# A decoder step on one core: memory keys of the sample group turned through DRAM beside other stages, and two steps of the memory heads moved to ScalarE

## Chip, core and metric

One core of a Trainium2 chip runs the whole kernel. The metric is the device time of one execution in microseconds. TensorE (PE) multiplies, VectorE (DVE) and ScalarE (ACT) do elementwise work, GpSimd (POOL) adds squares and issues DMAs, SyncE (SP) issues the DMAs of the weights. PSUM holds eight banks, in two tensors of four: `acc` for products, `ab` for everything else.

## What is computed

A decoder step for 256 prompt tokens and 8 sample tokens (264 columns together), model width 2048, two layers: a pooling mixer, memory attention and a SwiGLU; then dilated attention, memory attention and a SwiGLU. This case is about the memory attention:

```python
def _mem_attend(h, mk, mv, w_q, w_o):
    n, length, _ = h.shape
    q = (h @ w_q).reshape(n, length, MEM_HEADS, MEM_HEAD_DIM)          # 4 heads of 128
    sc = jnp.einsum('nlhd,nmhd->nhlm', q, mk).astype(jnp.float32) * (MEM_HEAD_DIM ** -0.5)
    p = jax.nn.softmax(sc, axis=-1).astype(mv.dtype)                   # over 256 memory rows
    o = jnp.einsum('nhlm,nmhd->nlhd', p, mv).reshape(n, length, MEM_DIM)
    return o @ w_o
```

It is called once with the prompt's memory keys, which the kernel computes itself, and once with `cache_mem_k[l]`, eight batches of 256 rows x 4 heads x 128 read from DRAM. The scores contract over the 128 of a head, so the cached keys, which lie as rows, are needed turned: 128 on the partitions, memory rows along the free dimension.

## The kernel before

**Weights.** All weight products take three matmuls of 128 x 128 with 264 columns: a weight block is rounded (`whi`) and its rest kept (`wlo`), and likewise the activations; high x high, high x low and low x high are added up. SyncE loads 1 MB blocks into four slots of `raw`; ScalarE rounds each half (`hi`, line 482), VectorE subtracts (`lo`, line 1367), TensorE multiplies (`products`, lines 819 to 821). A slot is loaded again when TensorE has used it (`half_used`). A `pair_item` is one output pair: 2 blocks, 96 matmuls, two banks of `acc`. VectorE and ScalarE run in a hand-written order in which `upto(n)` means "split all blocks up to n now"; `N0[name]` is the first block of a phase, `G0[name]` its first output pair.

**Pooling output** (`wout`): eight pairs. After each, VectorE adds it to `x` (`add_x`, line 1422), splits on, and makes the low part of the next layer's activations (`low_tiles`, line 1416); ScalarE makes the high part and the squares (`squares`, line 534); POOL adds the squares up (`add_squares`, line 2050).

**Memory attention** (`mem_attention`, called by `mem_layer` for each layer): two pairs of queries (`mq`), and between and after their halves, on TensorE, a list of steps: `scores(h)` of the prompt heads into `ab[0:2]`, softmax on VectorE and ScalarE, `turn_probabilities(h)` (four transposes into `ab[2]`), VectorE's copy of that bank to `PTm` (line 1680), `weigh(h)` with the values, VectorE's rounding and splitting of the head's output (`head_out`, lines 1646 and 1648). For the samples: `turn_keys(b)` for eight batches (eight transposes of 128 x 128 each, line 998, ScalarE copying two banks to `KTm(b)`, line 559), `sample_scores(q)` (line 1008), softmax, `turn_samples`, `sample_values(q)` (line 1029), `turn_outputs`. Then the output product `mo`. The cached key rows come in four loads of 1 MB: the first two during the pooling output (layer 0) or after the dilated heads (layer 1), the others by `load_memory_rows`; the value rows come when the query pairs are done, half from POOL and half from SyncE.

**FFN**: loops over gate/up pairs (`f0g0`, `f0g1`, `f0g2`) and down pairs. In the second part (`part == 1`) of layer 0 VectorE already turns, in each round of two pairs, rows of the window keys in 32 x 32 blocks (line 1790), POOL having loaded them to `rows_in` and then storing them to DRAM in `k_turned` in runs of 32 numbers, so that they lie turned there; `load_keys` (line 2123) reads them back. Rows and turned rows lie in `kx`.

Of the kernel before, what the change touches and what calls it, by code (L numbers as in the profile page):

```python
# [27 lines left out]
P = 128  # L28
# [55 lines left out]
for _l in range(2):  # L84
    CACHED += [((f"mk{_l}", i), s) for i, s in enumerate((9, 10, 5, 9))]
    CACHED += [((f"mv{_l}", i), s) for i, s in enumerate((0, 1, 2, 3))]
# [14 lines left out]
KT0 = {"m0": 0, "m1": TS}  # L101
# [9 lines left out]
def trunk(nc, a, o):  # L111
# [3 lines left out]
    with ctx:  # L115
# [58 lines left out]

        rows_in, rows_turned = kx[:, 0:NG * MEMD], kx[:, NG * MEMD:2 * NG * MEMD]
# [79 lines left out]
        kt_ready, kt_free = sem("kt_ready"), sem("kt_free")  # L255
# [12 lines left out]
        vs_done = sem("vs_done")  # L268
        inverse_ready, scales_ready = sem("inverse_ready"), sem("scales_ready")
# [205 lines left out]
        def _(eng):  # L475
# [79 lines left out]
            def memory_keys_turned(l, b):  # L555

                eng.wait_ge(kt_ready, KT0[f"m{l}"] + b + 1)
                src = ab[:, 0:2, :] if b < 4 else acc[:, 2 * (G0[f"mq{l}"] % 2):2 * (G0[f"mq{l}"] % 2) + 2, :]
                nc.scalar.copy(KTm(b).rearrange("p h j -> p (h j)"), src.rearrange("p b c -> p (b c)")).then_inc(kt_free, 1)
# [12 lines left out]
            def mem_attention(l):  # L572
# [22 lines left out]
                samples_exp(1)  # L595

# [207 lines left out]
        def _(eng):  # L804
# [147 lines left out]
            def mem_attention(l):  # L952

                n, g = N0[f"mq{l}"], G0[f"mq{l}"]
                h0, k0 = H0[f"m{l}"], KT0[f"m{l}"]
                sc, vo = 2 * (g % 2), 2 * ((g + 1) % 2)

                def scores(h):
                    eng.wait_ge(acc_free, g + h // 2 + 1)
                    if h == 0:  # L960
                        eng.wait_ge(kt_free, k0 + 4)
# [7 lines left out]
                def turn_probabilities(h):  # L969
# [5 lines left out]
                    last.then_inc(t_ready, 1)  # L975

                def weigh(h):
                    following(eng, pt_ready)
# [5 lines left out]
                    last.then_inc(o_ready, 1)  # L984

                def turn_keys(b):
                    key = (f"mk{l}", b // 2)
                    cached_landed(eng, key)
                    if b == 4:
                        eng.wait_ge(acc_free, g + 1)  # L990
                    elif b:
                        eng.wait_ge(kt_free, k0 + b)
                    rows = cached(key).rearrange("p (b k c) -> p b k c", b=2, k=2)
                    for h in range(NH_MEM):
                        for k in range(2):
                            j = 2 * h + k
                            dst = (ab[:, j // 4] if b < 4 else acc[:, sc + j // 4])[:, (j % 4) * P:(j % 4 + 1) * P]
                            last = nc.tensor.transpose(dst, rows[:, b % 2, k, h * P:(h + 1) * P], ident[:, :])  # L998
                    last.then_inc(kt_ready, 1)
# [36 lines left out]
                def turn_outputs(q):  # L1036
# [3 lines left out]
                pair_item(n, g, 2, xtile, xs_wait(f"memq{l}"), after_first=lambda: statistics(f"memq{l}"),  # L1040
                          halves={b: lambda b=b: turn_keys(b) for b in range(4)})
# [316 lines left out]
        def _(eng):  # L1358
# [260 lines left out]
            for j in range(8):  # L1619
# [588 lines left out]
```

## Time and profile before

| | us |
|---|---|
| device time, median of 3 runs | 2315.42 |
| lowest and highest | 2315.04 and 2316.87 |
| the profiled execution | 2315.27 |
| its span in the trace | 2313.5 |
| TensorE busy in it | 2298.4 (99%) |
| VectorE busy | 1345.1 (58%) |
| ScalarE busy | 955.4 (41%) |
| POOL busy | 163.7 (7%) |

The span is what lies between the first and the last instruction of the trace; some 1.8 us of the execution lie around it. TensorE's clock was granted in full throughout the span (0.999 on the mean). Busy times of matmuls overlap, as they are pipelined; the chain that ended last counts each only up to the start of the next.

### The profile page before, as it was taken

What the parts mean: (1) busy time and instruction counts of PE and PEld (TensorE: products, weight loads), DVE (VectorE), ACT (ScalarE), POOL (GpSimd) and SP (SyncE); (2) the same over time, 40 slices, a digit from 0 to 9 for tenths busy, and PEclk for the clock granted to TensorE, in tenths of its full rate; (3) what the DMA queues carried; (4) which work ended last, traced back from release to release, by engine and by line L of the source; (5) the groups of instructions that cost most, each with busy time, mean ns of one, the idle gap of its engine ahead of it and who ended that gap; (6) DMA issues with size and microseconds to landing.
All of it is one profiled execution on the core that took longest, in us unless ns stands there. A gap on an engine that the chain in (4) does not pass through costs nothing.

```text
span 2313.5 us, 45948 instructions
## 1 busy us (share of the span) xinstructions
PE 2298.4 (99%) x19092; PEld 2270.4 (98%) x19092; DVE 1345.1 (58%) x1717; ACT 955.4 (41%) x1143; POOL 163.7 (7%) x186
## 2 busy tenths in 40 slices
PE   9999999999999999999999999999999999999999
PEld 8999998999999999999999998899999999999999
DVE  7778557655446565455556776675554455544554
ACT  7434455433333333334444334553333333333333
POOL 0100112000001221000110111110000000000001
PEclk9999999999999999999999999999999999999999
DMA  8665765655557888555565675655555565555553
GB/s 292 196 196 177 242 197 181 194 181 180 177 179 235 246 248 246 180 181 178 176 192 174 201 224 180 217 165 181 181 178 177 181 181 178 178 179 182 178 170 126
DMA packets 385079, 445.88 MB, mean 193 GB/s; under 512 B 14762, under 2 KB 346810, under 8 KB 384446
## 3 DMA queue, kind: packets, MB, share of 16 engines
q1 hardware_dynamic: 371854, 401.72, 55.3%
q0 software_dynamic: 12592, 42.14, 6.4%
q8 instruction: 78, 1.28, 0.2%
q10 hardware_dynamic: 528, 0.52, 0.1%
q14 instruction: 27, 0.22, 0.0%
HBM read 432.50 MB, written 12.74 MB: 192 GB/s over the span
## 4 chain that ended last, share of the span: by engine, by line
PE 98%; DVE 1%; ACT 1%; DMA 0%; issue 0%; DVEq 0%; POOL 0%; ACTq 0%; POOLq 0%
PE acc L819 30%; PE acc L821 30%; PE acc L820 30%; PE acc L896 1%; PE acc L904 1%; PE acc L897 1%; PE ab L1076 0%; DVE wlo L1367 0%; PE acc L1029 0%; PE acc L998 0%; PE acc L1008 0%; PE ab L915 0%; PE ab L998 0%; PE ab L965 0%; DMA att<-in_norm_ffn 0%; PE ab L1112 0%
## 5 line engine op out<-in xcount | busy, mean ns | idle before, releaser
L819 PE MATMUL acc<-xs,whi 128*128 128x264 f32 (+1 forms) x3776 | 1081.3, 286 | 0.0
L821 PE MATMUL acc<-xs,wlo 128*128 128x264 f32 (+1 forms) x3776 | 1073.1, 284 | 0.0
L820 PE MATMUL acc<-xs,whi 128*128 128x264 f32 (+1 forms) x3776 | 1072.1, 284 | 0.0
L482 ACT ACTIVATE whi<-raw 128x1024 fp32r<-128x1024 f32 x744 | 763.1, 1055 | 704.1 <-DMA raw<-in_ffn_w_up 286.8
L1367 DVE TENSOR_TENSOR wlo<-raw,whi 128x1024 fp32r<-128x1024 f32 x744 | 875.9, 1228 | 210.2 <-ACT whi L482 189.5
L821 PEld LDWEIGHTS acc<-xs,wlo 128*128 128x128 f32 x3776 | 713.1, 189 | 0.0
L819 PEld LDWEIGHTS acc<-xs,whi 128*128 128x128 f32 x3776 | 709.2, 188 | 2.0 <-issue 1.1
L820 PEld LDWEIGHTS acc<-xs,whi 128*128 128x128 f32 x3776 | 710.7, 188 | 0.2
L819 PE MATMUL acc<-hA,whi 128*128 128x264 f32 (+1 forms) x1216 | 346.9, 285 | 2.5 <-DVE hA L1656 1.0
L821 PE MATMUL acc<-hA,wlo 128*128 128x264 f32 (+1 forms) x1216 | 345.6, 284 | 0.0
L820 PE MATMUL acc<-hA,whi 128*128 128x264 f32 (+1 forms) x1216 | 344.7, 283 | 0.0
L819 PE MATMUL acc<-hB,whi 128*128 128x264 f32 (+1 forms) x832 | 236.9, 285 | 0.0
L821 PE MATMUL acc<-hB,wlo 128*128 128x264 f32 (+1 forms) x832 | 236.4, 284 | 0.0
L820 PE MATMUL acc<-hB,whi 128*128 128x264 f32 (+1 forms) x832 | 236.0, 284 | 0.0
L819 PEld LDWEIGHTS acc<-hA,whi 128*128 128x128 f32 x1216 | 228.4, 188 | 3.5 <-DVE hA L1656 1.4
L821 PEld LDWEIGHTS acc<-hA,wlo 128*128 128x128 f32 x1216 | 229.1, 188 | 0.0
L820 PEld LDWEIGHTS acc<-hA,whi 128*128 128x128 f32 x1216 | 228.6, 188 | 0.0
L608 ACT ACTIVATE tmp<-tmp 128x528 f32<-128x528 f32 x44 | 28.4, 646 | 334.5 <-DVE tmp L1777 334.5
L821 PEld LDWEIGHTS acc<-hB,wlo 128*128 128x128 f32 x832 | 157.0, 189 | 0.0
L820 PEld LDWEIGHTS acc<-hB,whi 128*128 128x128 f32 x832 | 156.5, 188 | 0.0
L819 PEld LDWEIGHTS acc<-hB,whi 128*128 128x128 f32 x832 | 156.3, 188 | 0.0
L2050 POOL TENSOR_TENSOR ssq<-ssq,sq 128x528 f32<-128x528 f32 x41 | 56.9, 1388 | 1209.5 <-ACT sq L534 1209.5
(296 smaller groups left out, 1155.0 us busy)
## 6 DMA issues: line engine op xcount, KB each, us to landing
raw<-in_ffn_w_gate SPq DMA_DIRECT2D x176, 512.0 KB, 3.5
raw<-in_ffn_w_up SPq DMA_DIRECT2D x176, 512.0 KB, 3.5
raw<-in_ffn_w_down SPq DMA_DIRECT2D x176, 512.0 KB, 3.6
raw<-in_dil_w_q SPq DMA_DIRECT2D x48, 512.0 KB, 3.8
raw<-in_pool_w_in SPq DMA_DIRECT2D x32, 512.0 KB, 3.6
raw<-in_pool_w_out SPq DMA_DIRECT2D x32, 512.0 KB, 3.6
raw<-in_mem_w_v SPq DMA_DIRECT2D x16, 512.0 KB, 7.7
raw<-in_mem_w_k SPq DMA_DIRECT2D x16, 512.0 KB, 5.6
```

The lines of the kernel that those rows point to most:

```text
L482: nc.scalar.activation(half_block(whi, n, half), half_block(raw, n, half), ACT.Copy).then_inc(hi_ready, 1)
L608: nc.scalar.activation(siluF, gateF, ACT.Silu).then_inc(silu_ready, 1)
L819: mm(out, w_hi, hi_, start=first, stop=False)
L820: mm(out, w_hi, lo_, start=False, stop=False)
L821: return mm(out, w_lo, hi_, start=False, stop=last)
L896: mm(acc[:, 2 * (g % 2) + c, :], x_hi, w_hi, start=i == k == 0, stop=False)
L897: mm(acc[:, 2 * (g % 2) + c, :], x_lo, w_hi, start=False, stop=False)
L904: last = mm(acc[:, 2 * (g % 2) + c, :], x_hi, w_lo, start=False, stop=i == 3 and k == 3)
L1367: v.tensor_tensor(half_block(wlo, n, half), half_block(raw, n, half), half_block(whi, n, half).bitcast(F32), ALU.subtract).then_inc(lo_rea ...
L2050: gp.tensor_tensor(ssq[:, :, :], ssq[:, :, :], sq[:, :, :], ALU.add).then_inc(sq_added, 1)
```

## The change

- The sample group's memory keys are no longer turned by TensorE. Each 1 MB block of rows is loaded to `kx`, turned in 32 x 32 blocks by VectorE (one transpose of 2048 columns), and stored by POOL in four DMAs to `m_turned` in DRAM, in runs of 32 numbers, so that the keys lie turned there. Four blocks of layer 0 go through beside the pairs 0, 2, 4 and 6 of the pooling output, four of layer 1 beside the last four rounds of layer 0's first FFN part. POOL waits for the stores of a block before it loads the next.
- The turned keys come back in 256 KB loads, four per block: layer 0's sixteen when all four blocks are stored and the queries have begun, layer 1's first twelve after the dilated heads and four in the queries. The sample scores wait for two blocks each.
- ScalarE instead of VectorE copies the turned probabilities of the heads (`head_copied`) and rounds the head outputs (`head_high`); VectorE still subtracts. TensorE's order after the query pairs changes: the second sample scores come before the turning of head 2.
- The window keys' counts are shifted by eight blocks.

```diff
@@ memory, ScalarE
+        memory_rows_in, memory_rows_turned = kx[:, 0:BLK], kx[:, BLK:2 * BLK]
+        m_turned = nc.dram_tensor("m_turned", (2 * 4 * BLK, P), F32, kind="Internal").ap()
...
             def memory_queries(l):
-                n = N0[f"mq{l}"]
-                memory_keys_turned(l, 0)
-                upto(n + 2)
-                memory_keys_turned(l, 1)
+                upto(N0[f"mq{l}"] + 2)
                 root(STAT[f"memq{l}"])
-                upto(n + 3)
-                memory_keys_turned(l, 2)
-                memory_keys_turned(l, 3)
+                upto(N0[f"mq{l}"] + 3)
...
+                def head_copied(h):
+                    eng.wait_ge(heads_turned, 4 * l + h + 1)
+                    nc.scalar.copy(PTm[:, :, :].rearrange("p k t -> p (k t)"), ab[:, 2, :]).then_inc(heads_copied, 1)
+
+                def head_high(h):
+                    eng.wait_ge(heads_out, 4 * l + h + 1)
+                    src = acc[:, 2 * ((G0[f"mq{l}"] + 1) % 2) + 1, 0:TP] if h % 2 else ab[:, 3, 0:TP]
+                    nc.scalar.activation(hA[:, h, 0, 0:TP], src, ACT.Copy).then_inc(heads_high, 1)
+
                 upto(mo)
                 head_exp(0)
                 head_exp(1)
-                memory_keys_turned(l, 4)
+                head_copied(0)
                 upto(mo + 1)
-                for b in range(5, TS):
-                    memory_keys_turned(l, b)
+                head_copied(1)
+                head_high(0)
                 head_exp(2)
                 head_exp(3)
-                upto(mo + 2)
+                head_high(1)
+                head_copied(2)
                 samples_exp(0)
                 samples_exp(1)
+                head_copied(3)
+                head_high(2)
+                head_high(3)
+                upto(mo + 2)
@@ TensorE, mem_attention
                 def weigh(h):
-                    following(eng, pt_ready)
+                    eng.wait_ge(heads_copied, 4 * l + h + 1)
...
                 def sample_scores(q):
                     eng.wait_ge(qz_ready, l + 1)
-                    eng.wait_ge(kt_free, k0 + TS)
+                    for i in (2 * q, 2 * q + 1):
+                        eng.wait_ge(memory_keys_in[i], 64 * (l + 1))
...
-                pair_item(n, g, 2, xtile, xs_wait(f"memq{l}"), after_first=lambda: statistics(f"memq{l}"),
-                          halves={b: lambda b=b: turn_keys(b) for b in range(4)})
+                pair_item(n, g, 2, xtile, xs_wait(f"memq{l}"), after_first=lambda: statistics(f"memq{l}"))
                 pair_item(n + 2, g + 1, 2, xtile,
-                          halves={0: lambda: (scores(0), scores(1)), 1: lambda: turn_keys(4),
-                                  2: lambda: (turn_probabilities(0), turn_keys(5)), 3: lambda: turn_keys(6)})
+                          halves={0: lambda: (scores(0), scores(1)), 2: lambda: turn_probabilities(0)})
                 weigh(0)
-                turn_keys(7)
                 turn_probabilities(1)
                 scores(2)
                 scores(3)
                 sample_scores(0)
                 weigh(1)
+                sample_scores(1)
                 turn_probabilities(2)
-                sample_scores(1)
                 weigh(2)
                 turn_probabilities(3)
+                weigh(3)
                 turn_samples(0)
-                weigh(3)
                 turn_samples(1)
                 sample_values(0)
@@ VectorE: pooling output, heads, FFN
                 low_tiles("memq0", 2 * j)
+                if j % 2 == 0:
+                    eng.wait_ge(rows_landed, 8 * j + 16)
+                    v.transpose(memory_rows_turned, memory_rows_in).then_inc(keys_blocked, 1)
...
                 def head_finish(h):
-                    following(eng, o_ready)
-                    head_out(h, acc[:, 2 * ((g + 1) % 2) + 1, 0:TP] if h % 2 else ab[:, 3, 0:TP])
+                    eng.wait_ge(heads_high, 4 * l + h + 1)
+                    src = acc[:, 2 * ((g + 1) % 2) + 1, 0:TP] if h % 2 else ab[:, 3, 0:TP]
+                    v.tensor_tensor(hA[:, h, 1, 0:TP], src, hA[:, h, 0, 0:TP].bitcast(F32), ALU.subtract).then_inc(h_ready, 1)
...
                         split_h(h, t, upF)
                         eng.drain()
+                        if l == 0 and part == 0 and h is hB:
+                            eng.wait_ge(rows_landed, 16 * i + 16)
+                            v.transpose(memory_rows_turned, memory_rows_in).then_inc(keys_blocked, 1)
@@ POOL
+            def turn_memory_rows(l, i):
+                count = 4 * l + i
+                if count:
+                    eng.wait_ge(keys_stored, 64 * count)
+                src = a["cache_mem_k"][l, 2 * i:2 * i + 2]
+                eng.dma_start(memory_rows_in.rearrange("p (b k c) -> p b k c", b=2, k=2),
+                              src.rearrange("b (k p) h d -> p b k (h d)", p=P)).then_inc(rows_landed, 16)
+
+            def store_memory_rows(l, i):
+                eng.wait_ge(keys_blocked, 4 * l + i + 1)
+                rows = m_turned[(4 * l + i) * BLK:(4 * l + i + 1) * BLK, :].rearrange("(x t) (j s) -> t j x s", t=32, s=32)
+                for j in range(4):
+                    eng.dma_start(rows[:, j], quadrant(memory_rows_turned, j).rearrange("t (x s) -> t x s", s=32)).then_inc(keys_stored, 16)
+
+            def load_memory_keys(l, i):
+                for b in (2 * i, 2 * i + 1):
+                    for k in range(2):
+                        at = (4 * l + i) * BLK + (2 * (b % 2) + k) * MEMD
+                        eng.dma_start(KTm(b)[:, :, k * P:(k + 1) * P],
+                                      m_turned[at:at + MEMD, :].rearrange("(h d) j -> d h j", d=P)).then_inc(memory_keys_in[i], 16)
...
-            load_first_keys(0)
-            add_squares("memq0")
+            turn_memory_rows(0, 0)
+            for j in range(8):
+                if j:
+                    eng.wait_ge(sq_ready, j + 1)
+                    gp.tensor_tensor(ssq[:, :, :], ssq[:, :, :], sq[:, :, :], ALU.add).then_inc(sq_added, 1)
+                    eng.drain()
+                if j % 2 == 0:
+                    store_memory_rows(0, j // 2)
+                    if j < 6:
+                        turn_memory_rows(0, j // 2 + 1)
...
+            eng.wait_ge(keys_stored, 64 * 4)
+            load_memory_keys(0, 0)
             load_memory_rows(0)
             add_squares("ffn0")
+            for i in range(4):
+                turn_memory_rows(1, i)
+                store_memory_rows(1, i)
...
-            load_first_keys(1)
+            eng.wait_ge(h_ready, H0["m1"])
+            for i in range(3):
+                load_memory_keys(1, i)
             add_squares("memq1")
             load_memory_rows(1)
```

## Rows read from the trace of the kernel before

**Rows 1.** Page, part 1: busy us, share of the span, instructions.

```profile
PE 2298.4 (99%) x19092; PEld 2270.4 (98%) x19092; DVE 1345.1 (58%) x1717; ACT 955.4 (41%) x1143; POOL 163.7 (7%) x186
```

**Rows 2.** Waits of TensorE, whole span: us in total, times, longest.

```profile
PE ab L1151 <- DVE hA L1934: 2.0, 1, 2.0
```

**Rows 3.** Chain that ended last: start, us, what it is.

```profile
324.47 0.12 PE acc L821
324.59 0.87 PE ab L998 x8
...
360.06 1.06 PE acc L983 x4
361.12 0.44 PE ab L973 x4
```

**Rows 4.** Timeline of TensorE, layer 0: start, us, instruction, [idle before, releaser].

```profile
354.99 1.07 PE L998 MATMUL acc<-ident,kv_flat 128*128 128x128 f32 x8 [0.33 <-ACT hA_flat L559]
...
365.73 1.13 PE L983 MATMUL acc<-tmp,mV 128*128 128x256 f32 x4 [0.56 <-DVE tmp L1680]
...
367.01 1.93 PE L1029 MATMUL acc<-xs_flat,tmp 128*4 128x128 f32 x64
...
372.76 0.39 PE L819 MATMUL acc<-hA,whi 128*128 128x264 f32 x1 [0.52 <-DVE hA L1656]
```

**Rows 5.** Timelines of ScalarE and VectorE, memory attention and last heads.

```profile
346.70 2.01 ACT L482 ACTIVATE whi<-raw 128x1024 fp32r<-128x1024 f32 x2
...
1412.57 0.48 ACT L761 COPY tmp<-ab 128x384 f32<-128x384 f32 x1 [3.52 <-PE ab L1151]
...
347.80 2.36 DVE L1367 TENSOR_TENSOR wlo<-raw,whi 128x1024 fp32r<-128x1024 f32 x2 [2.24 <-ACT whi L482]
...
356.52 0.69 DVE L1680 COPY tmp<-ab 128x512 f32<-128x512 f32 x1 [0.91 <-PE ab L973]
```

**Rows 6.** Timeline of POOL, one round of the window keys.

```profile
729.29 3.69 POOL L2118 DMA_DIRECT2D k_turned<-kx  x4 [11.23 <-DVE kx L1790]
739.45 1.65 POOL L2114 DMA_DIRECT2D kx<-in_cache_win_k  x3 [6.47 <-DMA k_turned<-kx]
```

**Rows 7.** DMA issues: tile, queue, count, KB each, us to landing.

```profile
hA_flat<-in_cache_mem_k POOLq DMA_DIRECT2D x2, 1024.0 KB, 6.7
...
kv_flat<-in_cache_mem_k POOLq DMA_DIRECT2D x4, 1024.0 KB, 9.1
...
xs_flat<-in_cache_mem_v POOLq DMA_DIRECT2D x4, 1024.0 KB, 12.9
```

**Rows 8.** Timeline of VectorE: a round of FFN part 1; a pooling output pair.

```profile
724.81 0.71 DVE L1784 TENSOR_TENSOR tmp<-acc,tmp 128x528 f32<-128x528 f32 x1 [3.90 <-PE acc L821]
...
727.22 1.78 DVE L1790 STREAM_TRANSPOSE kx<-kx 128x1536 f32<-128x1536 f32 x1 [0.18 <-issue]
...
274.87 0.71 DVE L1422 TENSOR_TENSOR x<-acc,x 128x528 f32<-128x528 f32 x1 [1.37 <-PE acc L821]
...
281.43 2.35 DVE L1367 TENSOR_TENSOR wlo<-raw,whi 128x1024 fp32r<-128x1024 f32 x2
```

**Rows 9.** Windows of two pairs: busy by engine, PEclk, DMA share, GB/s last.

```profile
653.00:676.40 23.40, 23.40 (x194) 23.40 (x193) 10.67 (x10) 8.62 (x9) 0.00 (x0) 1.00 0.58 180
723.40:746.80 23.40, 23.40 (x195) 23.40 (x193) 14.10 (x14) 8.92 (x10) 5.33 (x7) 1.00 0.83 254
```

**Rows 10.** DMA from 878 to 895 us: queue, packets, MB, share; issues.

```profile
q0 software_dynamic: 848, 3.03, 61.9%
...
raw<-in_ffn_w_down SPq DMA_DIRECT2D x6, 512.0 KB, 10.6
```

**Rows 11.** Timelines of POOL and ScalarE: value loads; layer 1's first keys; third square.

```profile
353.22 1.49 POOL L368 DMA_DIRECT2D xs_flat<-in_cache_mem_v  x2 [22.89 <-PE acc L821]
...
1419.53 0.76 POOL L368 DMA_DIRECT2D kv_flat<-in_cache_mem_k  x1 [36.35 <-DVE hA L1934]
...
1430.07 0.63 ACT L534 ACTIVATE sq<-x 128x528 f32<-128x528 f32 x1
```

More of the change, by code:

```diff
@@ L84 @@
 for _l in range(2):
-    CACHED += [((f"mk{_l}", i), s) for i, s in enumerate((9, 10, 5, 9))]
     CACHED += [((f"mv{_l}", i), s) for i, s in enumerate((0, 1, 2, 3))]
@@ L254, in trunk @@
         scored = sem("scored")
-        kt_ready, kt_free = sem("kt_ready"), sem("kt_free")
+        memory_keys_in = [sem(f"memory_keys_in{i}") for i in range(4)]
         qz_ready = sem("qz_ready")
@@ L268, in trunk @@
         vs_done = sem("vs_done")
+        heads_turned, heads_copied, heads_out, heads_high = (sem("heads_turned"), sem("heads_copied"), sem("heads_out"),
+                                                             sem("heads_high"))
         inverse_ready, scales_ready = sem("inverse_ready"), sem("scales_ready")
@@ L954, in mem_attention @@
                 n, g = N0[f"mq{l}"], G0[f"mq{l}"]
-                h0, k0 = H0[f"m{l}"], KT0[f"m{l}"]
+                h0 = H0[f"m{l}"]
                 sc, vo = 2 * (g % 2), 2 * ((g + 1) % 2)
@@ L974, in turn_probabilities @@
                                                        Pm[:, h % 2, q, k * P:(k + 1) * P], ident[:, :])
-                    last.then_inc(t_ready, 1)
+                    last.then_inc(heads_turned, 1)
                 def weigh(h):
-                    following(eng, pt_ready)
+                    eng.wait_ge(heads_copied, 4 * l + h + 1)
                     if h >= 2:
@@ L983, in weigh @@
                         last = mm(out, mV[:, l, k, h * P:(h + 1) * P], PTm[:, k, :], start=k == 0, stop=k == 1)
[L984 to L999, printed above, removed]
+                    last.then_inc(heads_out, 1)
                 def sample_scores(q):
                     eng.wait_ge(qz_ready, l + 1)
-                    eng.wait_ge(kt_free, k0 + TS)
+                    for i in (2 * q, 2 * q + 1):
+                        eng.wait_ge(memory_keys_in[i], 64 * (l + 1))
                     for h in range(NH_MEM):
@@ L1729, in mem_attention @@
                 head_probabilities(2)
+                head_finish(1)
                 head_probabilities(3)
                 samples_max(0)
-                head_finish(1)
-                head_turned()
+                samples_max(1)
                 samples_probabilities(0)
-                samples_max(1)
-                head_turned()
+                samples_probabilities(1)
                 samples_turned(0)
-                samples_probabilities(1)
                 head_finish(2)
@@ L2057, in taken @@
                 eng.wait_ge(acc_free, g + 1)
+            def turn_memory_rows(l, i):
[16 more added lines that the diff above has]
+                                      m_turned[at:at + MEMD, :].rearrange("(h d) j -> d h j", d=P)).then_inc(memory_keys_in[i], 16)
             def load_memory_rows(l):
                 eng.wait_ge(half_used, 2 * N0[f"mq{l}"])
-                load_cached(eng, (f"mk{l}", 2))
-                eng.wait_ge(kt_ready, KT0[f"m{l}"] + 2)
-                load_cached(eng, (f"mk{l}", 3))
+                for i in (3,) if l else (1, 2, 3):
+                    load_memory_keys(l, i)
                 eng.wait_ge(half_used, 2 * (N0[f"mq{l}"] + 4))
@@ L2067, in load_memory_rows @@
                     load_cached(eng, (f"mv{l}", i))
-            def load_first_keys(l):
-                if l == 0:
-                    eng.wait_ge(stored[0], STORED[2])
-                    eng.wait_ge(stored[1], STORED[3])
-                else:
-                    eng.wait_ge(h_ready, H0["m1"])
-                for i in range(2):
-                    load_cached(eng, (f"mk{l}", i))
             def quadrant(rows, j, first=0, n=32):
@@ L2101, in _ @@
             eng.dma_start(pool_s[0, :, 0:NST - 1, :], a["state_pool"][0, :, 1:NST, :]).then_inc(out_done, 16)
-            load_first_keys(0)
-            add_squares("memq0")
+            turn_memory_rows(0, 0)
[8 more added lines that the diff above has]
+                        turn_memory_rows(0, j // 2 + 1)
+            gp.tensor_tensor(ssq[:, 0, :], ssq[:, 0, :], ssq[:, 1, :], ALU.add).then_inc(sq_added, 1)
+            eng.drain()
+            eng.wait_ge(keys_stored, 64 * 4)
+            load_memory_keys(0, 0)
             load_memory_rows(0)
             add_squares("ffn0")
+            for i in range(4):
+                turn_memory_rows(1, i)
+                store_memory_rows(1, i)
             def natural_rows(of, g, cols, b):
```

21 lines of the change are left out of this document (4 added, 17 removed).

## The prediction

> **What bounds the kernel now.** The page's first part comes first: TensorE is busy 99% of the span [rows 1]. The waits of TensorE over the whole span come second: the longest is 2.0 us [rows 2], the others are below it and few. So the span is TensorE's work laid end to end; an instruction taken from it is worth its own time, provided that no new wait opens where it stood. The chain that ended last comes third, as it gives the step from one instruction to the next (the busy time of a pipelined matmul does not): a weight product advances the chain by 0.12 us, the eight transposes of one batch's memory keys by 0.87 us [rows 3]. 16 such pieces stand in it, eight per layer. Last comes the timeline of layer 0's memory attention: there TensorE waits only before the last turning of keys (0.33), the last weighting of values (0.56) and, at its end, before the first output product [rows 4].
>
> **What is taken from TensorE.** 16 x 0.87 = 13.9 us, with nothing put in its place. Two of the waits go or are recounted below: 0.33 + 0.56 per layer, 1.8 us in all.
>
> **What the removed transposes covered.** They stood between steps of the softmax. I shift the rows of layer 0 forward and see who is late. With six pieces gone from the two query pairs, the second ends 5.2 us earlier, with the score and statistics steps unchanged. Four new waits follow. (1) The third head's scores need the second query pair, which VectorE scales after splitting the second output block; ScalarE rounds that block (2.01) after the new copy of the first turned probabilities, and VectorE's split takes 2.36, its second half after ScalarE's [rows 5]. Before, both stood ahead of the end of the pair; now the split ends 1.2 us after it and the scaling 1.9, while TensorE has a weighting (1.06) and a turning (0.44) to do [rows 3]: 0.4, with the hand-over 0.5 us. (2), (3) The weightings of heads 2 and 3 now follow their own turning directly, since the sample scores that stood between for head 2 have moved ahead. Each waits for a turning to drain and for ScalarE's copy of 512 columns. This copy isn't in the trace: the bounds are 0.48 (384 columns on ScalarE) and 0.69 (the same 512 columns on VectorE) [rows 5]; I take 0.58, nearer to the engine's own row, and with the drain each wait is 0.85. (4) The first sample values wait 0.35 for VectorE's copy of the turned sample probabilities, which had a weighting in between. Sum 2.55 us per layer. The rounding of the head outputs goes from VectorE to ScalarE behind the exponentials; it is beside the sample scores, and nothing on TensorE asks for heads 0 and 1 before them. Were that cover gone, a wait would cost one ScalarE instruction, about 0.5 us. Per layer: 8 x 0.87 + 0.89 - 2.55 = 5.3 us gained; both layers 10.6. With no new wait it would be 15.7, with all of them doubled 5.5.
>
> **What is put on the queues, layer 0.** POOL now makes a round trip per 1 MB block: load rows, VectorE transposes, four stores, wait for them, next load. It has one per two output pairs, 23.4 us. The nearest rows are the same trip for the window keys, 768 KB: four issues 3.69, landed 6.47 later [rows 6]. For 1 MB the issue is 4/3, 4.9, and the landing 6.5 (a latency) to 8.6 (bytes): 11.4 to 13.5; I take 12, since those stores had not filled the DMA engines. The issue of the load takes 0.8 and its landing 6.7 to 9.1 [rows 7]; I take 7.5, as it is alone in its queue. VectorE's transpose is 1.78 x 2048/1536 = 2.4 [rows 8]. The trip: 12 + 0.8 + 7.5 + 2.4 = 22.7, below 23.4, so rows lie ready when VectorE comes; from 11.4 + 0.8 + 6.7 + 2.4 = 21.3 to 13.5 + 0.8 + 9.1 + 2.4 = 25.8.
>
> VectorE waits in order, so a late row would hold back everything queued behind it: the splitting of the next weight blocks and, a pair later, the addition to x that frees banks. Cover, FFN: the transpose starts 2.4 us after the pair's last product [rows 8], with its 2.4 and a half split (1.2) behind it 6.0; TensorE needs that half 11.7 us (96 x 0.122) after the pair. 5.7 us are free. Cover, pooling output: the place of the transpose is 6.6 us after the pair's addition [rows 8], the split behind it ends 4.7 later, needed at 17.5: 6.2, less if the next addition is late; I take 5. A trip that is longer than 23.4 is late by the difference once, twice, three times at blocks 1, 2, 3. So TensorE loses nothing up to a trip of 25.1, and at 25.8 about 2 us in each of the two stages. I enter 0.
>
> A rule of the Trainium skill speaks against these stores: "DMA: Bandwidth & Descriptors", Specifications, has transfers below 512 B done by read-modify-write and short of line rate, and the runs here are 128 B. What that means for the landing is in the 6.47 us of the row already; whether it gets worse with more bytes in flight is the third rival's matter.
>
> The DMA engines: the weights alone fill 0.58 of them at 180 GB/s, with the window trip 0.83 [rows 9]. The new trip moves 4/3 of that: 0.58 + 0.25 x 4/3 = 0.91. TensorE did not idle in the window stretch; I enter 0 here too.
>
> **The loads back.** In layer 0 the sixteen 256 KB loads start when block 3 is stored. It belongs to pair 6, whose addition is at 274.87 + 3 x 11.7 = 310.0 [rows 8]; its transpose has its place at 316.6, ends at 319 and is stored by 331. 16 issues take 0.55 to 0.92 each [rows 6], 9 to 15 us. While such loads in 512-byte runs ran beside weights, POOL's queue moved 3.03 MB in 17 us (178 GB/s) and weights landed 10.6 us after issue [rows 10]. 4.2 MB at 178 GB/s is 23.6 us, till 354.6; where the weights pause, faster. The second sample scores stood at 361.12 + 0.44 [rows 3]; less eight pieces (6.96), a wait (0.33) and the turning now behind them (0.44), with the new wait of 0.5, they stand at 354.3. So the wait is 0 (loads at 300 GB/s) to 8 us (block 3 seven us later); I take 1.0. The memory values behind them: issued at the end of the query pairs as before, 13.8 us ahead of their use [rows 4, 11], landing 12.9 [rows 7]; the use moves by 1.74 + 0.89 - 2.55, nearly nothing, against that gate. In layer 0 they queue behind the keys, which the 1.0 includes.
>
> By the same page, Anatomy of one DMA (SWDGE path), a DMA costs about 2.0 us and a further 1 us per 436 KB: 4.2 MB in a row would then be down 12 us after the first issue, by 343, and the 1.0 us would be 0, the time 2304.7. The row with 178 GB/s beside weights disagrees, and I go by the row.
>
> **Layer 1** loads three blocks with 12 issues at 0.55 to 0.92, 7 to 11 us, from 1419.5, in front of the sums of squares on POOL. The first sum, which ScalarE's third square waits for at 1430.07 [rows 11], then comes at 1428 to 1432; a delay of 2 us to ScalarE's rounding lies within a cover like that of the pooling outputs (5), as additions and splits alternate there in the same way. Entered at 0. The keys have 60 us to land.
>
> **Sum.** 10.6 - 1.0 = 9.6. The profiled execution took 2315.27 (its span 2313.5 and 1.8 around it), 0.15 below the median of the runs: 2315.27 - 9.6 = 2305.7.
>
> **The rivals.** *Keys late in layer 0.* Block 3 is stored some us later than I put it, and the sample scores wait for loads that share the engines with weights and values: 8 us instead of 1: 2312.7. For it: 178 GB/s and 10.6 us [rows 10]; against: the loads need only half their blocks for the first scores. *Thin cover.* The softmax steps alone set the attention's time, the waits are double what I reckon: 10.6 becomes 5.5, with the key wait 2310.8. For it: every step there is a hand-over; against: their durations are all in the trace. *The round trip is longer than two pairs* (slower). At 0.91 of the DMA engines landings stretch as those of the weights did, and the trip is 27.5: 4.1 us late per block, 12.3 at the third, less 5 of cover: 7.3 in the pooling outputs, about as much in the FFN, and 5 more for layer 0's keys, 19.6 - and 2315.27 - 9.6 + 19.6 = 2325.3. It decides from a trip of 25.1. For it: [rows 9, 10] and the 128-byte runs; against: stores and loads alternate, so the queue is never deep. That the transposes do not leave TensorE can't be: no code issues them.
>
> **How the numbers follow.** Forecast 0.59, keys late 0.17, thin cover 0.11, long trip 0.13. A measurement of this kernel can tell about 0.2% (4.6 us) from no change: below 2310.8 is faster, above 2319.9 slower. Faster: 0.59 + half of thin cover + 0.04 of keys late = 0.68; slower: most of the long trip, 0.12; the same: 0.20. The forecast's own range is 2303 (fewer waits, keys in time) to 2309. The range for 8 in 10 reaches past both middle rivals: 2302.5 to 2317.
>
> **What would show it.** Right: no key transposes on TensorE; the stretch from the first query product to the first output product 5 to 6 us shorter in both layers; TensorE waiting for ScalarE's copies under 1 us each; POOL's store-to-store distance 23.4 us in the pooling output and the first FFN, with VectorE not waiting for rows. Wrong: VectorE idle before the memory-row transposes, longer from block to block (long trip); a wait of the sample scores for key loads (keys late); waits over 1.5 us per turning (thin cover).

## The result

| | before | after |
|---|---|---|
| median, us | 2316.57 (12 runs, 2315.0 to 2316.9) | 2321.23 (12 runs, 2318.0 to 2324.9) |
| profiled execution, us | 2315.27 | 2319.68 |
| its span, us | 2313.5 | 2317.9 |

After over before: 1.0022, 95% interval 1.0014 to 1.0030. The change makes the kernel slower by 4.7 us, where 9.6 us less were forecast. It lies above the upper end of the range, 2317. Two of e9's eleven executions took 3724 and 5756 us and are left out of its figures below.

The first part of the page of after answers [rows 1]:

```profile
PE 2289.4 (99%) x18964; PEld 2260.3 (98%) x18964; DVE 1355.2 (58%) x1709; ACT 947.9 (41%) x1143; POOL 222.8 (10%) x250
```

TensorE has 128 instructions fewer (16 times 8), as the change says. Its busy time fell by 9 us and the span grew by 4.4: TensorE is idle for 13 us more. The waits of TensorE over the whole span, which answer [rows 2] (us in total, times, longest):

```profile
PE ab L945 <- POOL ssq L2110: 4.8, 1, 4.8
PE acc L824 <- DVE x L1408: 3.2, 2, 1.8
PE ab L945 <- POOL ssq L2038: 2.4, 1, 2.4
PE ab L1137 <- DVE hA L1919: 2.0, 1, 2.0
PE ab L986 <- ACT tmp L577: 1.4, 2, 0.7
PE acc L986 <- ACT tmp L577: 1.3, 2, 0.7
```

The 2.0 us at the head of the list before are now the fourth row; it is the same wait (L1151 there, L1137 here). The three rows above it are new or have grown, and none is in the attention. The first and the third are the statistics of the memory queries: TensorE waits for POOL's last addition of squares. The fifth and sixth are the waits for ScalarE's copies that the prediction expected, below 1 us each.

The timeline of TensorE in layer 0, which answers [rows 4] (start, us, instruction, [idle before, releaser]):

```profile
321.65 0.28 PE L824 MATMUL acc<-xs,whi 128*128 128x264 f32 x1
...
332.48 1.25 PE L945 MATMUL ab<-ssq,ones 128*128 128x264 f32 x2 [4.81 <-POOL ssq L2110]
...
357.05 1.99 PE L968 MATMUL ab<-mKT,att 128*128 128x256 f32 x8 [0.43 <-DVE att L1654]
...
365.04 1.13 PE L986 MATMUL ab<-tmp,mV 128*128 128x256 f32 x4 [0.67 <-ACT tmp L577]
...
367.29 1.13 PE L986 MATMUL acc<-tmp,mV 128*128 128x256 f32 x4 [0.68 <-ACT tmp L577]
...
374.38 0.39 PE L824 MATMUL acc<-hA,whi 128*128 128x264 f32 x1 [0.52 <-DVE hA L1645]
```

The first query product starts 0.15 us later than before (321.50 in the trace of before): that is all that the traffic beside the pooling outputs cost TensorE. Then come 4.81 us of waiting, and the statistics matmuls behind it take 1.25. In a kernel below, where nothing was waited for, the same two take 0.61. The clock had fallen. The windows of after show it (length, PE busy and count, granted clock, DMA share, GB/s):

```profile
330.00:335.00 5.00, 2.52 (x9) 0.59 0.44 147
335.00:340.00 5.00, 5.00 (x33) 0.72 0.92 290
1402.00:1407.00 5.00, 5.00 (x31) 0.66 0.00 2
1445.00:1450.00 5.00, 3.19 (x15) 0.71 0.43 133
```

A mean of 0.59 to 0.72 is a stretch partly at the lower level (1.2 GHz). In all three places TensorE had just waited: 4.81, 2.01 and 1.82 us. Here each of these waits is paid twice; other waits of the same length were not (last section).

What POOL does meanwhile, at the end of the pooling outputs:

```profile
320.09 4.20 POOL L2058 DMA_DIRECT2D m_turned<-kx  x4 [3.22 <-DVE kx L1615]
324.30 1.34 POOL L2104 TENSOR_TENSOR ssq<-ssq,sq 128x528 f32<-128x528 f32 x1
331.69 0.74 POOL L2110 TENSOR_TENSOR ssq<-ssq 128x264 f32<-128x264 f32 x1 [6.05 <-issue]
```

The last two rows are the point of the case. The seventh addition ends at 325.64. The last one needs nothing but that, and begins 6.05 us later, with the releaser "issue": the profile shows nothing that it waited for. Between the two stands `eng.drain()`, as it did before, where this gap was 0.16:

```profile
325.45 0.76 POOL L2053 TENSOR_TENSOR ssq<-ssq 128x264 f32<-128x264 f32 x1 [0.16 <-issue]
```

What is new is that four stores were issued just ahead. The same in layer 1, on POOL, ScalarE and TensorE, beside [rows 11]:

```profile
1422.81 2.98 POOL L2065 DMA_DIRECT2D kx<-m_turned  x4 [37.97 <-DVE hA L1919]
...
1431.71 1.78 POOL L2035 TENSOR_TENSOR ssq<-ssq,sq 128x528 f32<-128x528 f32 x1
1440.45 1.31 POOL L2035 TENSOR_TENSOR ssq<-ssq,sq 128x528 f32<-128x528 f32 x1 [6.96 <-issue]
...
1441.86 0.65 ACT L536 ACTIVATE sq<-x 128x528 f32<-128x528 f32 x1 [6.09 <-POOL ssq L2035]
...
1433.01 0.39 PE L824 MATMUL acc<-hA,whi 128*128 128x264 f32 x1 [1.39 <-DVE x L1408]
...
1446.81 0.39 PE L824 MATMUL acc<-hA,whi 128*128 128x264 f32 x1 [1.82 <-DVE x L1408]
...
1468.55 0.71 PE L945 MATMUL ab<-ssq,ones 128*128 128x264 f32 x2 [2.38 <-POOL ssq L2038]
...
1508.09 0.39 PE L824 MATMUL acc<-hA,whi 128*128 128x264 f32 x1 [0.52 <-DVE hA L1645]
```

The first sum begins 8.9 us after the first of the twelve issues (1422.81 to 1431.71), as the prediction reckoned (7 to 11). The second comes 8.7 us after it. ScalarE's square waits 6.09 for that with its rounding of weights queued behind, and TensorE waits three times. The first of these waits (1.39) lies ahead of the second sum; it stands in e1 below too, and belongs to the issues.

**The account.** The waits come from the rows above. The price of the clock is the length of the same stretch here and in the kernel without these waits, each less its waits (e1 below for layer 0, e3 for layer 1). Layer 0: 4.81, and from statistics to first output product 41.90 against 39.65, so 2.25 for the clock; 7.1 in all. Dilated attention: the same wait of 2.01 us stands in both traces, the clock falls only in after's; after is 1.68 us behind before where the wait ends and 3.28 us at the end of the stretch, so 1.6. Layer 1: 0.45 (1.39 where 0.94 stood), 1.82, 2.38, and 1.8 for the clock; 6.5. With the 0.15 of the pooling outputs 15.3 us are lost. The span grew by 4.4, so 10.9 were gained: 5.6 of the 51.26 us of layer 0's stretch and 5.3 of the 84.39 of layer 1's. Forecast for this part: 10.6.

### The profile page after: what moved, and what is told of

Its sections match the earlier page's. It is cut to its first block, busy times and chain, and to the rows that moved or that the text cites. A ratio compares the mean times of both kernels' runs of the same rounds, so it can differ in the third digit from the quotient of the medians.

```text
span 2317.9 us, 45727 instructions
## 1 busy us (share of the span) xinstructions
PE 2289.4 (99%) x18964; PEld 2260.3 (98%) x18964; DVE 1355.2 (58%) x1709; ACT 947.9 (41%) x1143; POOL 222.8 (10%) x250
## 4 chain that ended last, share of the span: by engine, by line
PE 95%; issue 2%; DVE 1%; POOL 1%; ACT 1%; POOLq 1%; DMA 0%; DVEq 0%; ACTq 0%
PE acc L824 30%; PE acc L826 30%; PE acc L825 29%; PE acc L901 1%; PE acc L909 1%; PE acc L902 1%; DVE wlo L1353 1%; PE ab L1062 0%; POOLq L2036 0%; PE acc L1018 0%; PE ab L968 0%; PE acc L997 0%; PE ab L920 0%; ACT whi L484 0%; DMA att<-in_norm_ffn 0%
## 5 line engine op out<-in xcount | busy, mean ns | idle before, releaser
L2035 POOL TENSOR_TENSOR ssq<-ssq,sq 128x528 f32<-128x528 f32 x34 | 47.9, 1410 | 1132.5 <-ACT sq L536 1125.5
```

The lines of the kernel that those rows point to most:

```text
L2035: gp.tensor_tensor(ssq[:, :, :], ssq[:, :, :], sq[:, :, :], ALU.add).then_inc(sq_added, 1)
```

## The experiments

**Theory D**: a drain on POOL ends only when the transfers that POOL itself issued have landed, so an addition with a drain behind it holds back the next one for as long as they fly. **Rival P**: POOL is still busy writing out the transfers, for a time that goes by their number. **Rival Q**: the traffic itself, not the order on POOL, takes the time.

**e1_own_wait.** In the kernel after, each addition is followed by a wait for itself, in both places (arguments shortened):

```
  gp.tensor_tensor(ssq, ssq, sq, ALU.add).then_inc(sq_added, 1)
- eng.drain()
+ eng.wait_ge(sq_added, 8 * q + j)
```

> The changed kernel, only that POOL's drain after each addition of squares is replaced by a wait for that addition's own semaphore. Theory D (a POOL drain does not end before the DMAs that POOL has issued have landed): the 4.5 to 7 us between two additions behind DMA issues fall to under 1 us, TensorE no longer waits for statistics (4.8 and 2.4 us), its clock stays at 2.4 GHz after the first query block and in the dilated output, and the time is 2304 to 2308. Rival P (POOL is still writing descriptors, and the additions themselves are late): gaps and time stay, 2319 to 2323. Rival Q (the traffic of 16 MB more beside the weights holds back squares and weights): the same, 2319 to 2323.

Measured: 2310.14 us, ratio to before 0.9983 (0.9974 to 0.9992). By the ratios 0.39% or 9 us of after's time are gone, though the time lies 2 us above theory D's range. The traffic is unchanged, so rival Q falls as the main cause. Its trace, POOL and then TensorE:

```profile
324.24 1.33 POOL L2104 TENSOR_TENSOR ssq<-ssq,sq 128x528 f32<-128x528 f32 x1 [0.30 <-ACT sq L536]
325.64 1.62 POOL L2110 TENSOR_TENSOR ssq<-ssq 128x264 f32<-128x264 f32 x1
332.95 3.01 POOL L2065 DMA_DIRECT2D kx<-m_turned  x4 [5.69 <-DMA m_turned<-kx]
...
341.93 2.96 POOL L2065 DMA_DIRECT2D hA_flat<-m_turned  x4
...
327.61 0.61 PE L945 MATMUL ab<-ssq,ones 128*128 128x264 f32 x2
...
357.87 0.39 PE L997 MATMUL acc<-kx,att 128*4 128x256 f32 x2 [3.31 <-DMA hA_flat<-m_turned]
...
370.87 0.39 PE L824 MATMUL acc<-hA,whi 128*128 128x264 f32 x1 [0.52 <-DVE hA L1645]
```

The last sum follows the seventh at once, although the stores are still in flight (POOL then waits 5.69 us for them). The statistics wait for nothing. In their place stands a new wait of 3.31 us: the sample scores ask for keys whose loads were issued last, at 341.93. In after, TensorE came to its scores 7 us later (357.05 against 349.67), and the keys were there.

**e2_own_wait_layer0.** The same edit in the pooling outputs alone.

> As the run before, but the drains are replaced in the pooling output (layer 0) alone; those in front of layer 1 stay. Theory D: layer 0's wait for statistics (4.8) and the half clock behind it (2.6) go, layer 1's losses (some 6 us) stay: 2312 to 2315, half of what both bring. Rivals P and Q: 2319 to 2323. If nearly all of the gain shows here, layer 1's part was put down wrongly.

Measured: 2316.64, ratio 1.0006 (0.9998 to 1.0015), 1.6 us above theory D's range. Layer 0 has no wait for statistics, as in e1, and a key wait of 3.07; behind that the granted clock is 0.68 (357 to 362 us), where e1's stays at 1.00. Layer 1 looks as in after (waits of 1.41, 1.89 and 2.42, clock 0.73). The drains of layer 1 are the difference between e1 and e2: 6.5 us by the medians, 5.3 by the ratios, 5.4 in layer 1's stretch of the two traces. Those of layer 0 are the 0.16% (3.7 us) between e2's ratio and after's, net of the 3 us of keys that come to light.

**e3_layer1_sums_first.** All drains stay. In layer 1, POOL adds the squares before it issues the key loads:

```
- eng.wait_ge(h_ready, H0["m1"])
- for i in range(3): load_memory_keys(1, i)
  add_squares("memq1")
+ for i in range(3): load_memory_keys(1, i)
```

> The changed kernel with every drain kept; POOL adds layer 1's squares first and issues the twelve key loads of layer 1 behind them. Theory D and rival P both expect layer 1's additions 1.5 us apart with no wait of TensorE for its statistics, and 2313 to 2316 (6 us less), unless the later keys are waited for by the sample scores (then 1 to 5 us of it come back). Rival Q: the same traffic a little later, no gain: 2319 to 2323.

Measured: 2314.01, ratio 0.9992 (0.9983 to 1.0001), 0.30% or 7 us under after's. The waits in layer 1 are 0.93 and 0.27, where before has 0.94 and none; layer 0's wait for statistics stays, 6.98 in this trace. The drains cost nothing where no transfer stands ahead of them.

**e4_probe.** In the kernel before, executed once, POOL does extra work in an idle stretch: an addition, a drain, an addition, each time with other transfers issued just ahead. The last two have a wait for the addition itself in place of the drain. The timeline of POOL (L2112 are the additions; the issues are none, 4 KB, 1 MB, four of 256 KB in 128-byte runs, the same in long runs, 4 MB from DRAM to DRAM, and again the first four and the 4 MB):

> The kernel before, with two additions on POOL (a drain between them) put where POOL is idle in the first FFN, behind nothing, behind a DMA of 4 KB, a load of 1 MB (2 KB runs), four stores of 256 KB in 128-byte runs (8192 descriptors), the same four in 8 KB runs (128 descriptors), and a 4 MB copy within DRAM; then 128-byte stores and the 4 MB copy again with the wait for the first addition's own semaphore instead of the drain. Theory D: the gap between the additions is what is left of the landing: near 0.2 us behind nothing, 2 to 3 behind 4 KB, 5 to 8 behind 1 MB either way, the same for long and short runs, and well over 12 behind 4 MB; under 0.5 us with the own wait. Rival P: the gap goes by descriptors: 6 us for the short runs, under 1 us for the long ones and for the 4 KB.

```profile
403.74 1.85 POOL L2112 TENSOR_TENSOR kx<-kx 128x528 f32<-128x528 f32 x1 [0.16 <-issue]
406.25 0.57 POOL L2139 DMA_DIRECT2D m_turned<-kx  x1 [0.66 <-POOL kx L2112]
...
409.89 1.07 POOL L2112 TENSOR_TENSOR kx<-kx 128x528 f32<-128x528 f32 x1 [1.96 <-issue]
411.68 0.77 POOL L2123 DMA_DIRECT2D kx<-in_cache_mem_k  x1 [0.73 <-POOL kx L2112]
...
419.10 1.10 POOL L2112 TENSOR_TENSOR kx<-kx 128x528 f32<-128x528 f32 x1 [5.55 <-issue]
...
434.48 1.07 POOL L2112 TENSOR_TENSOR kx<-kx 128x528 f32<-128x528 f32 x1 [8.21 <-issue]
...
444.52 1.07 POOL L2112 TENSOR_TENSOR kx<-kx 128x528 f32<-128x528 f32 x1 [5.16 <-issue]
446.31 0.53 POOL L2143 DMA_DIRECT2D m_turned<-in_cache_mem_k  x1 [0.72 <-POOL kx L2112]
...
463.74 1.07 POOL L2112 TENSOR_TENSOR kx<-kx 128x528 f32<-128x528 f32 x1 [15.80 <-issue]
465.56 4.21 POOL L2132 DMA_DIRECT2D m_turned<-kx  x4 [0.75 <-POOL kx L2112]
469.77 3.51 POOL L2112 TENSOR_TENSOR kx<-kx 128x528 f32<-128x528 f32 x2
479.13 0.53 POOL L2143 DMA_DIRECT2D m_turned<-in_cache_mem_k  x1 [5.85 <-DMA m_turned<-kx]
```

And the landing of the three single transfers (issues, KB, us from issue to landing):

```profile
m_turned<-kx POOLq DMA_DIRECT2D x1, 4.0 KB, 3.5
kx<-in_cache_mem_k POOLq DMA_DIRECT2D x1, 1024.0 KB, 7.3
m_turned<-in_cache_mem_k POOLq DMA_DIRECT2D x1, 17.2
```

406.25 + 3.5 = 409.75, and the addition begins at 409.89; 411.68 + 7.3 = 418.98 and 419.10; 446.31 + 17.2 = 463.51 and 463.74. Behind a single transfer the drain ends 0.1 to 0.2 us after the landing, whatever the size and the kind. Behind four stores it is 0.3 us: the last of the short runs is issued at 424.1 and lands 10.0 later, of the long runs at 437.8 and 6.4; the additions begin at 434.48 and 444.52. Behind the twelve loads of layer 1 in after it is 0.9 (1430.9 + 8.6, and 1440.45). Short runs hold the drain 3 us longer than long ones, against theory D's forecast of the same, because they land that much later. One transfer of 4 MB holds it longest, so rival P falls. With the addition's own wait the two additions run one behind the other (469.77 to 473.28) while the stores have almost 6 us to fly. Theory D stands.

**e8_before_own_wait** is the control: the kernel before with own waits in place of its drains.

> The kernel before with the additions' own waits in place of the drains, nothing else. Theory D: there a drain stands behind unlanded transfers only once or twice and TensorE did not wait for the additions, so nothing changes: 2315.0 to 2316.0. Rival O, the own wait is cheaper as such and e1's 11 us over the changed kernel had little to do with transfers: 2311 to 2314.

Measured: 2316.54, 0.5 us above theory D's range; ratio 1.0002 (0.9993 to 1.0011). The own wait is worth nothing as such.

**e5_pair_waits.** What was left in e1 is the 3.31 us of keys. e1 with layer 0's loads waiting pair by pair (and no longer repeated in `load_memory_rows`):

```
- eng.wait_ge(keys_stored, 64 * 4)
- load_memory_keys(0, 0)
+ eng.wait_ge(half_used, 2 * N0["mq0"])
+ for i, stores in ((0, 1), (1, 2), (3, 4), (2, 4)):
+     eng.wait_ge(keys_stored, 64 * stores)
+     load_memory_keys(0, i)
```

> The kernel with the additions' own waits (e1, 2310.14 us), and layer 0's sixteen key loads no longer wait together for the last pair's stores: pairs 0 and 1 are loaded as soon as their own rows are stored, then pair 3, then pair 2. Theory K, late issue: the 3.31 us that TensorE waited in e1 for the keys in hA_flat came from the issue at 341.9, behind twelve loads that all stood behind the last store; pair 3 now issues near 333 and pair 2 near 336, the wait goes, some of it may come back as a wait for the cached values (0.30 in e1): 2306.5 to 2309. Rival S, the transfers are the bound (share 0.9 to 1.03 of 16 engines between 330 and 360 in e1): the same bytes land no earlier, the wait stays or moves: 2309.5 to 2311.

Measured: 2308.09, ratio 0.9968 (0.9956 to 0.9980). POOL issues the loads of pair 3 (hA_flat) at 336.40 in place of 341.93, and TensorE no longer waits for keys. Theory K, by the trace; by the time less surely, as the intervals of e1 and e5 overlap. The edit also puts pair 3 ahead of pair 2, which was not run apart. The traced execution took 2309.49: its last stores came 2.4 us later than e1's, and since the seventh addition is queued behind their 4.20 us of issue, the statistics waited 2.03.

```profile
322.12 4.20 POOL L2058 DMA_DIRECT2D m_turned<-kx  x4 [7.01 <-DVE kx L1615]
326.33 1.34 POOL L2104 TENSOR_TENSOR ssq<-ssq,sq 128x528 f32<-128x528 f32 x1
...
336.40 2.96 POOL L2065 DMA_DIRECT2D hA_flat<-m_turned  x4 [0.76 <-DMA m_turned<-kx]
```

**e7_both_orders** is e5 with e3's order in layer 1 on top.

> e5 with layer 1's seven additions ahead of its key loads (e3's order). Theory D with the issue time: the waits of 1.39 and 0.53 us in layer 1's queries fall to what before and e3 had, 0.94 and 0.27, so 0.7 us under e5: 2305.8 to 2308.3. Rival L, the keys become late in layer 1, as all sixteen loads now issue only from 1458 on and a load landed up to 13.6 us after its issue, while TensorE needs pairs 2 and 3 at 1484: 1 to 3 us over e5, with a wait of the sample scores on m_turned in the trace.

Measured: 2306.79, ratio 0.9959 (0.9945 to 0.9972), the lowest of the study: 8.5 us under the kernel before. From e5 it is not told apart by time. Layer 1's 1.39 is 0.93, as expected. The statistics there still wait 0.60, no less than in e1, so the 0.7 us are half shown. Keys are in time in both layers; the cached values, issued behind them, are waited for 0.91 and 0.74.

**e6_heads_on_vector** and **e10_heads_on_vector_again**: e1 with the copies of the turned probabilities and the rounding of the head outputs back on VectorE, keys still through DRAM (arguments shortened):

```
- nc.scalar.copy(PTm, ab[:, 2, :]).then_inc(heads_copied, 1)          # ScalarE, after heads_turned
+ v.tensor_copy(PTm, ab[:, 2, :]).then_inc(heads_copied, 1)           # VectorE, likewise
- nc.scalar.activation(hA[:, h, 0, 0:TP], src, ACT.Copy).then_inc(heads_high, 1)
+ head_out(h, src)                                                    # both halves on VectorE
```

> e1 with the copies of turned probabilities and the rounding of head outputs back on VectorE, in TensorE's new order; keys through DRAM stay. Theory H, the moves to ScalarE pay in the order without turns: with nothing left to stand between the heads, VectorE's maxima, normalizing and subtractions queue ahead of each copy, TensorE's waits in each layer's attention grow by 2 to 4 us over e1's 1.8: 2314 to 2318. Rival N, the moves are worth nothing and the gain is all the removed turns: 2309 to 2311.5.

> The kernel of e6 once more, for a second trace of it: its times stood 9 us over e1's, and e9 showed no price of heads on VectorE. Theory C, what e6's first trace held (2.06 us of statistics in layer 0 with half clock, the addition of 6.04 us) are accidents of one execution: this trace has neither, and its time is 2309 to 2314. Theory M, one of the two comes with this kernel: the trace shows it again, at 2316 to 2322. Theory X, something else that neither trace of e6 and e9 shows separates them.

Measured: e6 2319.39, ratio 1.0020 (1.0009 to 1.0031); e10 2317.22, ratio 1.0009 (0.9999 to 1.0020). By the time alone theory H is the nearer, though e6 lies 1.4 us above its range. The traces say otherwise: layer 1's attention, from statistics to first output product, takes 39.72 us in e6 and 39.59 in e10, against 39.73 in e1, with waits of 0.78 for VectorE's copies where e1 has 0.68 for ScalarE's. Layer 0's takes longer, 45.57 and 46.20 against 43.26, but the copies are 0.1 us each there too. The loss is in places that the edit doesn't touch. In e6's trace: 2.06 us of statistics in layer 0 with the granted clock at 0.67 behind it (330 to 335 us), keys 3.24 with the clock at 0.66 behind (360 to 365 us), and at the end of layer 1's output products this addition on POOL, beside four low parts on VectorE:

```profile
1529.30 6.04 POOL L2025 TENSOR_TENSOR ssq<-ssq,sq 128x528 f32<-128x528 f32 x1 [1.16 <-ACT sq L536]
...
1529.56 4.62 DVE L1336 TENSOR_TENSOR wlo<-raw,whi 128x1024 fp32r<-128x1024 f32 x4
```

It took 6.04 us where most take 1.33, about VectorE's 4.62 and its own 1.33 on end, and TensorE waited 4.1 for it. In e10's trace the same addition took 1.53, and there VectorE's four low parts took 6.31 in place of 4.62: one of the two engines waits for the other, and either can be the one. So the long addition does not come with every execution of the kernel. Layer 0 of e10 waited 5.33 for keys, with the clock at 0.59 behind (360 to 365 us). Theory C has e10's trace, as neither accident is in it, but not its time; that leaves theory X.

Late keys are in both traces, and most of the loss before layer 1 lies there: the first output product of layer 0 comes at 375.13 and 375.04, in e1 at 370.87. The last block's stores are issued at 322.26 and 321.54, in e1 at 319.74, and the last key loads at 346.48 and 345.70 in place of 341.93. These stores stand ahead of everything that the edit changes. In e5 and e7 they are as late (322.12 and 321.05), but the loads there do not all wait for them.

**e9_both_orders_heads_on_vector**: the same edit on e7, where keys are in time.

> e7 (2306.79 us) with the copies of turned probabilities and the rounding of head outputs back on VectorE, as in e6. In e6's trace layer 1's attention took 39.72 us from statistics to first output product against 39.73 in e1, and the time was lost elsewhere: 2.06 us of statistics in layer 0 with half clock, and an addition of 6.04 us on POOL at the end of layer 1's output products (1.33 elsewhere), beside four low parts of VectorE back to back, with 4.1 us of TensorE behind it. Theory C, these two are accidents of a run and the moves are worth nothing: 2306 to 2309, no addition over 2.5 us. Theory M, with the heads on VectorE its work stands so that it wins against POOL at that place in nearly every execution: the long addition is there again, layer 1's attention is again within 0.3 us of e7's, and the time is 2311 to 2316. Theory H, the moves pay in the attention itself: statistics to first output product grows by over 1 us in both layers.

Measured: 2308.58 over nine executions, ratio 0.9980 (0.9970 to 0.9989). No addition over 2.31. From statistics to first output product 39.43 us in layer 0 and 39.70 in layer 1 (e7: 40.58 and 40.42); less the waits for values 39.15 and 39.19 (e7: 39.67 and 39.68). Theory C holds for the attention, as these stretches did not grow: the moves to ScalarE bring it nothing that shows. For the whole it is less sure. By the ratios e9 is 0.2% slower than e7 (5 us; 1.8 by the medians), with intervals that just overlap, and the two traces are not alike: e9's execution is its fastest (2306.24), e7's is its slowest (2309.26) and has the clock fall in the dilated attention. A price of the heads on VectorE of up to some 0.4% is not excluded. That the price of e6 and e10 hangs on keys that are not in time is argued, from e9 with the same heads and keys in time; it is not shown. e1 has late keys too (3.31), and why the stores came later in e6 and e10 than in e1 stays open.

## Why the prediction was wrong

**The step that failed** is the one on layer 1, "Entered at 0": the twelve issues were taken as 7 to 11 us of POOL's time in front of the first sum, and the first sum came where the step put it. What it left out is the drain behind that sum, which holds the second for another 7 us, until the loads have landed. The term is 6.5 us, not 0 (the account: 6.5; e3: 7). The drain alone is 5.3 to 6.5 of it (e2 less e1); about 1 us are the issues, which e1 keeps (1.39 where 0.94 stood, 0.53 of statistics where none stood), so the cover was a little too small even for them. **The same omission in layer 0**: the step on the loads back follows blocks, issues and landings, and names the split of weights and the addition to x as what is queued behind VectorE's transposes, but never asks what is queued behind POOL's stores. It is the last two additions of squares, on which the statistics depend. That term is 7.1 us. The trace of before could not show the drain's price. In layer 0 nothing was in flight at the last drain (the gap of 0.16). In layer 1 two 1 MB loads were, but the later one landed near 1430.0 (issued at 1420.28, 9.7 to landing), 0.8 us before the second sum had its square and began, at 1430.78. The code could have raised the question, as a drain stood between an issue and a sum that TensorE needs.

**The clock** was in no term. Of the 15.3 us lost 5.7 are the clock behind the waits. In the dilated attention it fell behind a wait that was there before, of the same 2.01 us; the traces of before, e1, e2 and e8 show no fall at that place, those of after, e3, e5 and e7 do; nor do those of e6, e9 and e10, where the wait is 2.36. So this 1.6 is not shown to come from the change. What decides it stays open.

**What was right.** The transposes: 10.6 forecast for attention and removed work together, 10.9 found. The new waits: 0.5, 0.85 and 0.85 forecast, 0.43, 0.67 and 0.68 found; ScalarE's copy of 512 columns, put at 0.58, is 0.585. The fourth (0.35) didn't come. The round trip: stores 23.8 and 24.0 us apart (272.28, 296.07, 320.09) against 23.4, VectorE's transpose 2.31 against 2.4, VectorE's waits for rows 0.37 at most behind the first block, and the pooling outputs 0.15 us longer, so the long trip as the prediction told it did not happen.

**Half right: the loads back.** The 1.0 us had bounds of 0 and 8. In after the wait was 0, since TensorE came late itself; with the drains away it is 3.31 and 5.33 (e1, e10). Both lie between the forecast's 1.0 and the 8 of the rival of late keys, whose mechanism is the one that the rows show: the scores wait for loads; e5 adds that it is their issue behind the last store that makes them late. On the landing, the estimate from the page "DMA: Bandwidth & Descriptors" (Anatomy of one DMA) of the Trainium skill had all keys down 12 us after the first issue; the trace of e1 has the last 24.9 after it (332.95 to 357.87), with the engines full:

```profile
340.00:350.00 10.00, 9.57 (x76) 1.00 1.02 333
350.00:360.00 10.00, 6.69 (x79) 1.00 1.03 355
```

**Of the rivals** none named the mechanism. Slower was given 0.12, all of it to the round trip. With the drains replaced and the loads in order (e7) the time is 2306.8, 1.1 us from the forecast. That nearness is in part luck: the forecast's 1.0 for keys is not in e7's trace, and in its place stand 1.65 for values, 1.27 for statistics and 1.6 of clock in the dilated attention.

## What to carry to other kernels

When transfers are put on an engine's queue, list every wait and every drain that follows them on that engine, and ask of each drain what is in flight then. A drain on POOL behind its own transfers was a wait for them in all these runs; a wait on the semaphore of the one instruction that matters was not. And ask, where one wait lets four loads start, whether each of them needs all that is waited for: the pair-wise waits, with the pairs in another order, took the wait of 3.31 us for keys out of the trace and brought some 2 us.

## What the runs showed of the hardware

- A drain on POOL lasts until POOL's own transfers have landed, and ends 0.1 to 0.2 us after a single one, 0.3 after four and 0.9 after twelve: the gap between two additions was 0.16 us with nothing in flight, 1.96 with 4 KB, 5.55 with 1 MB, 15.80 with 4 MB from DRAM to DRAM (e4).
- Waits of TensorE of 1.82, 2.01 and 4.81 us were followed by stretches at the lower clock level that cost 1.6 to 2.3 us more. Not every wait was: behind 2.01 us in before and 3.31 us in e1 the granted clock stayed at 1.00, while behind 3.07 us at the same place in e2 it was 0.68.
- One addition on POOL took 6.04 us beside four operations of VectorE back to back, with two operands in SBUF each. "SBUF — State Buffer" of the Trainium skill (Who interferes with whom) says that such an operation and a GpSimd operation that reads SBUF exclude each other for a whole instruction. The row agrees, and shows that the addition was kept out for four in a row. In e10 at the same place the addition took 1.53 us and the four 6.31 in place of 4.62; by the profile the addition begins first in both traces, by 0.26 and 0.27 us.
- Most kernels with the round trip through DRAM beside the work scatter more: after lies within 6.9 us, e2 within 11.6, before within 1.9. But e3, which has the same round trip and only another order in layer 1, lies within 2.1, so the round trip alone does not make it.
